# A hybrid encoder block on one core: Y stored by chunk pairs behind the loads, x loaded ahead of the scan in two parts, decay over chunk pairs, the norm's sums of two tiles apart

## The reference

```python
h = rms_norm(x, ln1_g); p = h @ w_in                      # 2560 columns
r, k, v, wd, ad, gd = split(token_shift(p[:, :1792]))     # RWKV part, 8 heads x 64
q, ka, va = split(p[:, 1792:])                            # attention, 8 heads, 2 kv heads
decay = exp(-exp(w_log(wd)))                              # per direction z, token, channel
def step(S, t):                                           # one scan per direction
    Sa = S @ a_t
    S = S * w_t + outer(Sa, b_t) + outer(v_t, k_t)
    return S, S @ r_t
y = group_norm(ys[forward] + ys[backward]) * lnx_g + lnx_b
o_rwkv = (y + bonus) * gate
o_att = windowed_attention(q, ka, va, |t-s| <= 128, ALiBi, sink)
x = x + concat(o_rwkv, o_att) @ w_out
h = rms_norm(x, ln2_g)
x = x + (gelu(conv3(h @ w_gate)) * (h @ w_up)) @ w_down    # 2816 wide
return rms_norm(x, lnf_g)
```

## Time and profile before

| | |
|---|---|
| time, median of 3 runs | 1420.46 us (1416.09 to 1421.94) |
| the profiled execution | 1425.6 us, of which the span of its instructions is 1423.8 us |
| granted TensorE clock, mean | 0.954 of full |
| busy share | PE 91%, PE weight load 71%, DVE 61%, ACT 37%, POOL 17% |
| the chain that ended last | PE 69%, DVE 15%, DMA 6%, issue 4%, ACT 3%, SP's queue 2% |
| in the chain, DMA | work<-v_d 2%, work<-in_w_in 2% |
| data | 179.53 MB in 146854 packets, mean 126 GB/s |

### The profile page before, as it was taken

The page is one execution under the profiler, slowest core; times in us unless marked ns, Lnnn a source line. Parts: engine busy times, 40 slices in busy tenths (PEclk is TensorE's granted clock), DMA queues, the critical chain, the costliest instruction groups (busy, mean ns, idle before and its releaser), DMA issues.

```text
span 1423.8 us, 28423 instructions
## 1 busy us (share of the span) xinstructions
PE 1288.8 (91%) x11260; PEld 1005.3 (71%) x11260; DVE 872.6 (61%) x1093; ACT 522.2 (37%) x726; POOL 235.2 (17%) x247
## 2 busy tenths in 40 slices
PE   6999899995787888889878999999999998999996
PEld 2476677774565665568766888888888877888875
DVE  4977587797576788783378555556555563322345
ACT  3725435311354666741125333333333341211220
POOL 1000011041032143410103222222222110000000
PEclk9999999998589999999979999999999999999998
DMA  5046857885477687414201222222222354232103
GB/s 206 19 107 169 201 136 168 209 249 115 122 230 251 197 236 222 140 37 144 87 29 45 89 89 88 88 86 67 74 82 88 133 208 161 89 115 72 55 23 119
DMA packets 146854, 179.53 MB, mean 126 GB/s; under 512 B 53456, under 2 KB 108816, under 8 KB 146800
## 3 DMA queue, kind: packets, MB, share of 16 engines
q1 hardware_dynamic: 137408, 152.16, 36.1%
q0 software_dynamic: 4288, 12.98, 3.3%
q10 hardware_dynamic: 5104, 13.67, 2.8%
HBM read 121.16 MB, written 57.54 MB: 126 GB/s over the span
## 4 chain that ended last, share of the span: by engine, by line
PE 69%; DVE 15%; DMA 6%; issue 4%; ACT 3%; SPq 2%; POOL 0%; DVEq 0%; ACTq 0%; POOLq 0%
PE banks L1079 27%; PE banks L689 17%; PE banks L671 7%; PE banks L1114 5%; PE banks L677 3%; DMA work<-v_d 2%; DVE work L1903 2%; DVE work L1899 2%; DMA work<-in_w_in 2%; PE banks L653 1%; PE banks L930 1%; PE banks L879 1%; PE banks L968 1%; PE banks L869 1%; DVE op L1697 1%
## 5 line engine op out<-in xcount | busy, mean ns | idle before, releaser
L1079 PE MATMUL banks<-op,sw_hi 128*128 128x512 f32 x1176 | 363.4, 390 | 6.5 <-DVE hT L2128 4.2
L1079 PEld LDWEIGHTS banks<-op,sw_hi 128*128 128x128 f32 x1176 | 221.3, 188 | 53.9 <-DVE sw_lo L1697 5.7
L1079 PE MATMUL banks<-op,sw_lo 128*128 128x512 f32 x588 | 229.5, 390 | 0.0
L2078 DVE TENSOR_TENSOR xT<-xT,banks 128x1024 f32<-128x1024 f32 x24 | 29.3, 1220 | 170.2 <-PE banks L689 156.0
L1079 PEld LDWEIGHTS banks<-op,sw_lo 128*128 128x128 f32 x588 | 110.7, 188 | 23.0
L1423 ACT ACTIVATE sw_hi<-work 128x1024 fp32r<-128x1024 f32 (+1 forms) x63 | 75.9, 1204 | 122.6 <-PE banks L1079 111.8
L1697 DVE TENSOR_TENSOR sw_lo<-work,sw_hi 128x1024 fp32r<-128x1024 f32 (+1 forms) x63 | 89.9, 1428 | 39.4 <-ACT sw_hi L1423 39.3
L671 PE MATMUL banks<-ph_hi,pw_hi 128*128 128x512 f32 x272 | 87.7, 404 | 7.0 <-DVE pw_lo L1697 3.0
L1671 POOL TENSOR_TENSOR work<-work 128x512 f32<-128x512 f32 x21 | 27.1, 1292 | 395.9 <-DMA work<-in_w_gu 309.3
L671 PE MATMUL banks<-ph_hi,pw_lo 128*128 128x512 f32 x272 | 85.8, 397 | 0.0
L689 PE MATMUL banks<-g_hi,down_hi 128*128 128x512 f32 x256 | 79.7, 393 | 6.1 <-DVE down_lo L1697 4.2
(11 more groups left out here) (252 smaller groups left out, 2458.2 us busy)
## 6 DMA issues: line engine op xcount, KB each, us to landing
work<-scan_d SPq DMA_DIRECT2D x32, 768.0 KB, 4.8
work<-in_w_gu SPq DMA_DIRECT2D x88, 256.0 KB, 4.5
scan_d<-work SPq DMA_DIRECT2D x16, 1024.0 KB, 5.4
g_d<-hT SPq DMA_DIRECT2D x22, 512.0 KB, 2.9
scan_d<-work SPq DMA_DIRECT2D x32, 256.0 KB, 6.5
work<-in_w_down SPq DMA_DIRECT2D x16, 512.0 KB, 3.8
work<-in_w_in ACTq DMA_DIRECT2D x15, 512.0 KB, 3.8
work<-g_d SPq DMA_DIRECT2D x15, 512.0 KB, 4.5
```

The source lines that it names most:

```text
L1079: mm = pe.matmul(banks[:, 3 * slot + bank, :], w[:, n, k * P:(k + 1) * P], x[n][:, k, :], start=(opens and k == 0 and p_ == 0), stop=(k == ...
L2078: tt(x, x, product, ALU.add).then_inc(added[slot], 1)
```

## The change

Four things change.

- **Y by pairs.** ACT's Y copies of both chunks of a pair go into one buffer, `Ys[slot]` of twice the size (`y_move` picks the two quarters; slot 0's buffer lies elsewhere now). SP stores a pair with four DMAs instead of eight, and issues them behind `load_scan` instead of ahead of it. ACT waits for the store of the same slot one iteration back. ACT's wait for the inverses' moves comes at q = 2 of iteration 0 instead of q = 0. POOL waits for slot 0's last store before it writes `h_lo`.
- **x in two parts.** POOL issues three of the eight loads of x once `qkv_mm` is 6, ahead of its wait for the second half of the solve, and the other five right behind its stores of the last inverses. The old place in the scan is empty.
- **Decay over pairs.** The reset mask of the decay sums is set to 1 between the two chunks of a pair, so that the sums run on over a pair. The first chunk of a pair then needs no scaling of the state: DVE adds the update into S in place, and scales by `PC` only after the second chunk. PE waits for the scaled state (`S_new`) only at the first chunk of a pair; at the second the wait for `S_add`, which stands before L918 in both kernels, is enough. In the first stage DVE clears 16 columns of `L` after each `chunk_decay`, and POOL sets the mask once.
- **The norm's sums apart.** `y_variance` (at q = 0) and `y_mean` (at q = 2) of tile b = 0 stay ahead of DVE's copy of U, those of b = 1 move behind the state's add.

The diff, cut to its core (left out: the semaphore's name, and the end of the scan, where SP stores by pairs in the same way and ACT's and SP's counts are halved):

```diff
@@ -261,7 +261,7 @@
         St = w(2, NPAIR, HD)
         assert w.at == XG_AT + 2 * T
         w = Carve(XG_AT + 3 * T)
-        Ys = [w(2, NPAIR * HD) for _ in range(2)]
+        Ys = [Carve(WA_AT + 2 * WPART + 2 * NPAIR * HD)(2, 2, NPAIR * HD), w(2, 2, NPAIR * HD)]
         vs_last = Carve(XG_AT + 2 * T)(3, P)
         assert w.at == XG_AT + 4 * T
         AGB.append(w(2, 3, NPAIR, P))
@@ -288,6 +288,10 @@
             return (UV[slot].rearrange("p z c j i -> p z c (j i)")[rows, z, cc ^ z, :],
                     banks[rows, 2 - 2 * cc + z, 0:NPAIR * HD])
+        def y_move(slot, cc):
+            return Ys[slot].rearrange("p z c n -> p (z c) n")[:, cc:4 - cc:3 - 2 * cc, :]
         heads = lambda x: x.rearrange("p (h n) -> p h n", n=HD)
         by_head = lambda x: x.rearrange("p (e j) c -> p j e c", e=2)
         yn = oT[:, 0:NPAIR, :].rearrange("p j (n c) -> p j n c", c=P)
@@ -513,20 +517,19 @@
             load_inverses(1, 1)
             y_rows = y_d.rearrange("z (c t) (e n) -> z c e t n", t=C, e=2)
-            def store_y(i, q):
-                sp.wait_ge(s["Y_out"], 4 * i + q + 1 + FREE)
+            def store_y(i, slot):
+                sp.wait_ge(s["Y_out"], 4 * i + 2 * slot + 2 + FREE)
                 for z in range(2):
-                    c = 4 * i + q if z == 0 else i * -4 + (NC - 1 - q)
+                    c = 4 * i + 2 * slot if z == 0 else i * -4 + (NC - 2 - 2 * slot)
                     for e in range(2):
-                        sp.dma_start(y_rows[z, bass.ds(c, 1), e].rearrange("o t n -> (o t) n"),
-                                     Ys[q % 2][x_rows(e, z, C, C), z])\
-                          .then_inc(ys_stored[q % 2], 16)
+                        sp.dma_start(y_rows[z, bass.ds(c, 2), e].rearrange("c t n -> t c n"),
+                                     Ys[slot][x_rows(e, z, C, C), z]).then_inc(ys_stored[slot], 16)
             def load_y(r, tiles_):
                 for slot, n in enumerate(tiles_):
-                    sp.wait_ge(ys_stored[slot], 128 * r + 128 * YT + FREE)
+                    sp.wait_ge(ys_stored[slot], 64 * r + 64 * YT + FREE)
                 sp.sem_inc(passed, 1)
                 for slot, n in enumerate(tiles_):
                     sp.wait_ge(yin_used[slot], r + FREE)
@@ -540,17 +543,14 @@
                         if slot == 1:
                             sp.wait_ge(s["sc_mm"], 8 * i + 8)
                             load_qk(i + 1)
-                        store_y(i, 2 * slot)
-                        if slot == 1:
                             sp.wait_ge(s["sc_out"], 8 * i + 8)
                             load_distances(i + 1)
-                        store_y(i, 2 * slot + 1)
-                        if slot == 1:
                             sp.wait_ge(s["o_mm"], 2 * i + FREE)
                             load_values(i)
                         sp.wait_ge(s["Y_mm"], 4 * i + 2 * slot + 2)
                         sp.wait_ge(s["S_mm"], 4 * i + 2 * slot + 2)
                         load_scan(i + 1, slot)
+                        store_y(i, slot)
                     if first == YT - 1:
                         load_y(i - (YT - 1), (i * -1 + (NC // 4 - 1), i))
             def load_weights(slot, n, src, kn=KD):
@@ -921,7 +921,8 @@
                             if lead and q == 0 and j == NPAIR - 1:
                                 mm.then_inc(X_mm[z], 1)
                     if not (lead and q == 0):
-                        pe.wait_ge(s["S_new"], n + 1)
+                        if cc == 0:
+                            pe.wait_ge(s["S_new"], 2 * i + q // 2 + 1)
                         settled()
                     for j in () if lead and q == 0 else range(NPAIR):
                         for z, c2 in enumerate(c2s):
@@ -1345,12 +1346,12 @@
                             for b in range(2):
                                 y_square(2 * i + (b - 2 * YT), b)
                         act.wait_ge(s["Y_mm"], n + 1)
-                        if first == 0 and q == 0:
+                        if first == 0 and q == 2:
                             for moved in inverse_moved:
                                 act.wait_ge(moved, 16 * 2 * NPAIR)
                             act.wait_ge(s["TI1_stored"], 16 * 2 * NPAIR)
-                        act.wait_ge(ys_stored[q % 2], 64 * (2 * i + q // 2) + FREE)
-                        act.activation(Ys[q % 2][:, :, :], banks[:, 2 * cc:2 * cc + 2, 0:256], ACT.Copy).then_inc(s["Y_out"], 1)
+                        act.wait_ge(ys_stored[slot], 64 * i + FREE)
+                        act.activation(y_move(slot, cc), banks[:, 2 * cc:2 * cc + 2, 0:256], ACT.Copy).then_inc(s["Y_out"], 1)
                         if again and q == 0:
                             for b in range(2):
                                 y_root(2 * i + (b - 2 * YT - 2), b)
@@ -1565,6 +1566,7 @@
                 v = L[z].rearrange("p (c t) -> p c t", t=CP)
                 pool.memset(v[:, :, 0:1] if z == 0 else v[:, :, C:C + 1], 0.0).then_inc(s["zero_made"], 1)
             pool.wait_ge(s["consts_loaded"], 16 * NCONST)
+            pool.memset(reset.rearrange("p (c t) -> p c t", t=CP)[:, 1::2, 0], 1.0).then_inc(s["gaps_zero"], FREE)
             for q in range(4):
                 r = slice(32 * q, 32 * q + 32)
                 pool.wait_ge(s["zero_made"], 2 + q)
@@ -1599,11 +1601,19 @@
                     pool.dma_start(TI_d[0, e][:, :, j].rearrange("s c t -> c s t"), TI[0][C * j:C * (j + 1), e])\
                         .then_inc(s["TI_stored"], 16)
+            def x_load(tiles_):
+                for k in tiles_:
+                    pool.dma_start(xT[:, k, :], a["xT"][:, k, :]).then_inc(s["x_again"], 16)
+            pool.wait_ge(s["qkv_mm"], 6)
+            x_load(range(3))
             pool.wait_ge(s["sol_row"], 2 * (C - 1))
             for j in range(NPAIR):
                 for e in range(2):
                     pool.dma_start(TI_d[1, e][:, :, j].rearrange("s c t -> c s t"), TI[1][C * j:C * (j + 1), e])\
                         .then_inc(s["TI1_stored"], 16)
+            x_load(range(3, KD))
             pool.wait_ge(s["TI_stored"], 16 * 2 * NPAIR)
             pool.wait_ge(s["TI1_stored"], 16 * 2 * NPAIR)
@@ -1652,13 +1662,10 @@
                         for b in range(2):
                             y_centre(2 * i + (b - 2 * YT), b, again)
                     normalised(2 * i, 0)
-                if first == 1:
-                    pool.wait_ge(s["Y_mm"], 8)
-                    for k in range(KD):
-                        pool.dma_start(xT[:, k, :], a["xT"][:, k, :]).then_inc(s["x_again"], 16)
             for b, tile in enumerate((1, NC // 4 - 2)):
                 y_normalise(NT - 4 + b, tile, b)
+            pool.wait_ge(ys_stored[0], 64 * NC // 4 + FREE)
             for k in (4, 7):
                 pool.wait_ge(sp_s["att_hi"], KD + k - NPAIR + 1)
                 pool.tensor_tensor(h_lo[:, k, :], oT[:, k, :], h_hi[:, k, :].bitcast(F32), ALU.subtract)\
@@ -1799,6 +1806,7 @@
             def decay_sums(j, z):
                 dve.wait_ge(s["lora_sig"], 3 * j + (1, 3)[z])
+                dve.wait_ge(s["gaps_zero"], 2 * j + FREE)
                 order = slice(None) if z == 0 else slice(None, None, -1)
                 dve.tensor_tensor_scan(L[z][:, order], reset, L[z][:, order], 0.0, ALU.mult, ALU.add)\
                     .then_inc(s["L_ready"], 1)
@@ -1808,6 +1816,7 @@
                 in_step_order = slice(None) if z == 0 else slice(None, None, -1)
                 last = E[z].rearrange("p (c t) -> p c t", t=CP)[:, in_step_order, (C if z == 0 else 0)]
                 dve.tensor_copy(PC[:, z, bass.ds(j, 1), :].rearrange("p o c -> p (o c)"), last)
+                dve.memset(L[z].rearrange("p (c t) -> p c t", t=CP)[:, 1 - z::2, z * C], 0.0).then_inc(s["gaps_zero"], 1)
             def gram_rows(j, z):
@@ -1998,11 +2007,10 @@
                         earlier = first > 0 or g == 1
                         if cc == 0:
                             logits(i, g, (0,), earlier)
-                            for b in range(2):
-                                if again and q == 0:
-                                    y_variance(2 * i + (b - 2 * YT - 2), b)
-                                elif late and q == 2:
-                                    y_mean(2 * i + (b - 2 * YT), i + (1 - YT), b)
+                            if again and q == 0:
+                                y_variance(2 * i + (-2 * YT - 2), 0)
+                            elif late and q == 2:
+                                y_mean(2 * i + -2 * YT, i + (1 - YT), 0)
                         else:
                             logits(i, g, (3,), earlier)
                             half_maxima(i, g, 0)
@@ -2014,13 +2022,21 @@
                         else:
                             half_maxima(i, g, 1)
                         dve.wait_ge(s["S_mm"], n + 1)
-                        if first == 0 and q == 0:
-                            dve.wait_ge(s["S_new"], 1)
```

(18 more changed lines are left out.)

12 lines of the change are left out of this document (6 added, 6 removed).

## The result

The changed kernel took 1411.86 us (median of 18 runs, 1401.90 to 1414.60) against 1418.59 of the kernel before (18 runs on the same chip, 1408.82 to 1425.18): a ratio of 0.9938, 95% interval 0.992 to 0.9955. I had given 1409 and a range of 1402 to 1419. Six runs of the same kernel later gave 0.9906 (0.9879 to 0.9934). By these two comparisons it is 0.6 to 0.9% faster. The profiled execution took 1414.6 us, span 1412.4; before it was 1425.6 and 1423.8. So the two profiles differ by 11.0 us in time (forecast: 11.7) and the medians by 6.7, since the profiled execution of before lay further above its median (7.0 us, against 2.7 for the changed kernel's).

A forecast was written before the change was run, and what follows sets the result against it. TensorE bounds it, its scan waiting for loads, the copy of U and the scaled state. -9.7 - 3.9 - 2.2 + 2.1 + 2.0 = -11.7 us: 1425.6 to 1413.9 profiled, median 1409, range 1402 to 1419.

The forecast's parts named there:

- x out of the scan: In the scan, moving x's loads away ends one chunk's late operands and the previous chunk's wait for values: -9.7 us.
- Loads ahead of the stores: In the scan, operand loads issued 2.0 us earlier shorten TensorE's waits for them: -3.9 us (bounds 0 and -5.3).
- Decay over pairs: In the scan, sixteen state scalings go, saving only TensorE's uncovered waits: -2.2 us (bounds 0 and -11.0).
- The norm's sums and the later `load_y`: Iterations 5 to 7: Y's reload and POOL's add come later, delaying the copy of U: +2.1 us (-3.3 to +5.4).
- The opening: Start of the scan: five x tiles delay the small copies and the inverses' reload: +2.0 us (0 to +7.1).
- the upper bound: Start of the scan: the inverses' reload lands as late as operand loads did beside all eight x tiles: +7.1 us.
- the rule cited in the prediction: Trainium skill: DMA engines serve queues in turn; a completion counts only after that engine's earlier writes on any queue.
- a chance of gain alone: Iteration 1's 10.52 us chunk, begun by a TensorE issue stall, may go with earlier loads: -4.6 more, 1404; chance 0.14.

The follow-up runs named there:

- stores-first kernel: The changed kernel with each pair's Y stores issued ahead of the operand loads again; 1407.91 us, ratio 0.988 to the kernel before.
- late stores first: The changed kernel with slot 1's Y store ahead of the operand loads in SP's last loop only; 1404.98 us, ratio 0.9872 to before.
- second profile: The changed kernel run and profiled again with nothing changed, to see the scatter; 1410.83 us, ratio 0.9906 to before.
- two bursts: The changed kernel with direction z = 1's operand loads in iterations 0 and 1 held until the next chunk's state product; 1408.93 us, ratio 0.9902 to before.
- little loads: The changed kernel with the large operand loads in iterations 0 and 1 cut from 768 to 64 KB (output wrong); 1402.25 us, ratio 0.9849 to before.

## Why the prediction came out as it did

**x out of the scan** was right: -9.7 forecast, 9.4 when undone. Its other half, that three tiles beside the solve hold nothing up, can't be told from the scatter of the first add.

**Loads ahead of the stores** was right in place and size. No wait for v_d is left. At q = 1 of iteration 2 TensorE's Y product ends at 437.66 and the first operand load goes out at 437.88 (within 0.3, as said). At q = 3 it is 449.32 and 451.22, 1.9 us where I had said 1.6:

```profile
437.01 0.65 PE L978 MATMUL banks<-work 32*32 32x64 f32 x32
...
448.67 0.65 PE L978 MATMUL banks<-work 32*32 32x64 f32 x32
```
```profile
437.88 0.37 SPq L469 DMA_DIRECT2D work<-scan_d  x1
...
450.51 0.37 SPq L491 DMA_DIRECT2D work<-va_d  x1
451.22 0.35 SPq L469 DMA_DIRECT2D work<-scan_d  x1
```

Iteration 3 lost the 3.9 us it had too much. Undoing the order alone costs 2.2 us in iterations 2 to 4, less than that. The pairs need half as many stores as before, which would explain the rest; it was not tried by itself.

**Decay over pairs** came out near its size: -2.2 forecast, 2.7 when undone, of which 1.3 is clear of the scatter.

**The norm's sums and the later `load_y`** is a term that was mis-sized: +2.1 forecast, -2.2 for iterations 5 to 7 in the first profile and -3.3 in the second, with the decay's part in them (up to 1.5). Its mechanism held. `load_y` came 3.0 us later counted from the iteration's first state add (7.1 against 4.1), as forecast. POOL's add came 1.5 later instead of 2.3, and the copy of U 0.4 later (515.34, 13.9 us after the add, against 13.5), "no earlier", as said. The later reload costs 6.2 us by the stores-first kernel and 7.3 by late stores first, and I had 5.4 in three iterations. What I sized wrongly is the edit against it: I gave the moved mean 1.1 us each, 3.3 in all, and it was 5.6, since it was a wait for a second, later load that left the chain. And I had booked the gains of the other chunks at nothing. Chunk by chunk, the three with the means became longer by 1.0, 0.5 and 0.0 us, 1.5 together and near the +2.1; what I lacked was the rest, -3.7 us, of which -2.9 in the chunks right behind them (from q = 2 to q = 3). What in those gave it was not taken apart. (The reload at 514.9 plus 3.5 to 5.3 us also gives 518.4 to 520.2 for POOL's add, and not 518.6 to 520.3.)

**The opening** came out at the size given, in another place. ACT's copy of X and the reload of the inverses were no more than 0.3 us later counted from ACT's first issue (350.19, before 348.81), and so was the first add:

```profile
350.19 10.04 ACTq L1284 DMA_DIRECT2D work<-work  x8
360.35 0.38 ACT L1333 ACTIVATE work<-banks 128x256 f32<-128x256 f32 x1 [19.66 <-issue]
```
```profile
368.44 0.31 PE L954 MATMUL banks<-work 32*32 32x64 f32 x6 [0.76 <-DMA work<-work]
369.53 0.60 PE L954 MATMUL banks<-work 32*32 32x64 f32 x26 [0.79 <-issue]
```

The cost fell on the second chunk, whose inverses landed late (0.76) and whose instructions were late too (0.79): 7.6 us instead of 5.9 (8.2 in the second profile). That is +1.8 to +2.3 against a term of +2.0 for other reasons. The copies landed 1.7 us later in the median and not behind all five tiles, so the upper bound, to which the rule cited in the prediction had leaned, did not come true. That the clock would fall at the opening, to 0.50 behind the first add where it was 0.92 before, the prediction did not have either. The first add itself came 1.7 us later by the profile's clock, 1.4 of it ahead of ACT's first issue; this is within the scatter of that column.

**Iteration 1** is where the prediction failed, although its total came out. No term of the sum held it; it took 8.0 us more than before, 6.8 in the second profile. I had read the stall of TensorE's own issue at the earlier trace rows, called its cause unknown, and let it enter as a chance of gain alone. It should have been bounded on both sides: first-pass code under heavy operand loads, and a change that moves just those loads. Both criteria that I had set for a wrong forecast were met once: the first pair of iterations was longer by over 4 us in the first profile (+6.9) and not quite in the second (+3.9), and the late iterations were over 3 us away from before in the second (-3.3) and not in the first (-2.2). Part was made good there by a shorter iteration 0 behind its first chunk (-2.9 and -5.2). The forecast's total still held in the profile because this loss was met by -4.3 in the late iterations against their term, by a scattering last stretch (-2.9), and by iteration 0. That these cancelled is luck. In the median, 2.9 us above my 1409, it was met less.

Not settled is which part of the change makes the stalls worse. The order of stores and loads, x, the decay and the norm's sums were each undone alone, and iteration 1 stayed at 33.0 to 36.0 us against 29.3. The decay comes nearest: with it by chunk the three stalls sum to 5.2 us, against 8.4 and 8.7 in the changed kernel and 7.3 to 8.2 with one of the other parts undone. What all four have in common is storing Y by pairs, four DMAs where eight had been. Y by chunks in the new kernel was not tried, and of before there is but one profile.

## What to carry to other kernels

Size a moved wait by what it waits for: two loads that land one after the other cost the chain the second landing, unless the second's user stands behind the chain. One order of stores and loads needn't serve all iterations; here loads first is right until somebody reads the stores and wrong from then on, and the split was worth 6 to 7 us of the late iterations. In a loop's first pass, look at the instruction queue: a burst of loads that saturates the DMA engines can starve the engine's code. Cutting the burst in two took 6 to 9 us off the first two iterations in the profile, and with late stores first it took the whole time from 0.9872 to 0.9814 of before.

## What the hardware showed unexpectedly

- TensorE stalled 1.5 to 3.9 us at fixed instructions of code run for the first time; ahead of the two longest in the changed kernel, operand loads kept the DMA engines 0.94 and 0.98 busy for 5 us in which no 16 KB instruction block moved. Each stall ended 2.3 to 3.3 us after a block had moved. With two bursts the same stalls were 0.2 to 1.2 us. From 430 to 520 us, on repeated code, there were none at 243 GB/s.
- After such a stall the granted clock stood at 0.50 (1.2 GHz) with TensorE busy all the time from 402 to 405 us, so that a stall costs more than its length. An estimate: from the changed kernel to the one with little loads the three stalls shrink by 5.5 us in sum and iterations 0 and 1 by 11.2 us, about twice as much.
